# First modulation weights loaded in four column blocks, each block's tiles modulated and multiplied as it lands, tokens loaded first

## The chip, the cores and the metric

The kernel runs on one core of one Trainium2 chip. The metric is the device time of one execution in microseconds (us), from the first to the last instruction. The core has TensorE (PE; its weight loads are listed as PEld), VectorE (DVE), ScalarE (ACT), GpSimd (POOL) and SyncE (SP), which here issues the DMAs. Each engine has its own instruction stream and runs it in order; streams meet at semaphores, so an instruction that waits holds up all that stands behind it in its stream.

## What is computed

One inference step of a two-layer backbone over 512 latent tokens (`x_sample`, modulated by `c`) and 128 context tokens (`x_prompt`, modulated by `c_ctx`), width 1024, all in fp32. Only the first operation of the first layer is touched: tokens are normalised, scaled and shifted by two rows of a modulation that is itself a matrix product, and multiplied by the input projection.

```python
def modulation(cond, w_ada, b_ada):
    m = jax.nn.silu(cond) @ w_ada + b_ada          # w_ada: (1024, 6 * 1024)
    return m.reshape(cond.shape[0], 6, D_MODEL)

def modulate(x, g, shift, scale):
    return rms_norm(x, g) * (1 + scale[:, None, :]) + shift[:, None, :]

for layer in range(DEPTH):
    mc = modulation(c_ctx[None], w_ada[layer], b_ada[layer])
    ml = modulation(c, w_ada[layer], b_ada[layer])
    g = norm_gains[layer]
    hp = modulate(xp, g[0], mc[:, 0], mc[:, 1])
    hs = modulate(xs, g[0], ml[:, 0], ml[:, 1])
    ...                                            # h @ w_in, mixers, residuals, MLP
```

## The kernel before

**Layout.** Activations are held turned: 1024 features in KD = 8 tiles (k = 0 to 7) of 128 partitions, T = 640 tokens along the free dimension. The tokens are two halves of HALF = 320 columns: half (or part) 0 holds latent tokens only, half 1 the rest and the 128 context tokens, which have another scale and shift. Every fp32 matrix product is done as three fp32r matmuls over a split of each operand in a high and a low piece: lo x hi, hi x lo, hi x hi.

**Weights.** A piece of `w_in_ac` (128 output columns, all 8 k tiles, 512 KB) lands in one of four `stage` buffers; ACT copies it to `w_hi` (`act_split`, L566), DVE subtracts to `w_lo` (`dve_split`, L575). A unit is one piece times the tokens: 8 k tiles, two halves, three matmuls of 320 columns, so 48 matmuls. Units 0 to 2 are written by hand in `units_beside` (L863 to L865), units 3 to 19 come from `unit` (L824 to L826). Unit 3 needs the bank of unit 1, so ACT's copy of unit 1's result (L1594); ahead of that copy in ACT's stream stand the copy of unit 0 and the splits of pieces 4 and 5.

**The modulation.** The first two rows of the modulation (shift and scale, 2048 columns of `w_ada`, 8 MB) come as eight row blocks of 1 MB, one for each k (`ada_a`, L699). `ada_step(k)` (L912) is four matmuls of 512 columns with 32 weight columns each, which lie side by side in PE's columns. After the eighth, ACT copies the result (`modrow_a`, L1570), PE turns it (L953), DVE adds the bias (`first_columns`, L2115) and makes the coefficients (L2106).

**The operands.** For half 0 and tile k: DVE `modulate` (L2064), ACT high piece (L1505), DVE low piece (`low`, L2081). For half 1: DVE multiplies by the token factor (L2071), ACT applies scale and shift to the two groups (L1516, two instructions) and copies to the high piece (L1520), DVE subtracts for the low piece (L2088). The token factor itself is ACT's sum of squares (L1559) and root, spread over the partitions by PE (`spread_rows`, L935 and L937). Tokens are turned by PE (`turn_tokens`, L923) and copied by DVE (`turned_out`, L2173 and, for the context, L2175).

**The order of the DMAs.** All go through SP's queue: ident, the vectors (`vrow`, `brow`), `x_sample`, the eight `ada_a` blocks, pieces 0 and 1, `x_prompt`, pieces 2 and 3, small ones, then two slabs for the rest of the modulation (`slab_ac`) and the next pieces. The orders are written out by hand on every engine.

## Time and profile before

| | us |
|---|---|
| median of 3 runs (lowest, highest) | 1739.69 (1739.23, 1740.97) |
| the profiled execution | 1740.12 |
| its span | 1738.3 |
| last `ada_a` block used by PE | 32.8 |
| first product of unit 0 | 41.0 |
| first product of unit 3 | 67.8 |

Share of the span with the engine busy: PE 96%, PEld 86%, DVE 63%, ACT 42%, POOL 12%. The granted TensorE clock averages 0.98 of full speed. Times in the rows are microseconds from the span's start; DMA share is the mean busy share of the 16 DMA engines. A matmul's listed duration overlaps its neighbours', so PE's pace is read from the distance of two starts.

### The profile page before, as it was taken

What the parts mean: (1) busy time and instruction counts of PE and PEld (TensorE: products, weight loads), DVE (VectorE), ACT (ScalarE), POOL (GpSimd) and SP (SyncE); (2) the same over time, 40 slices, a digit from 0 to 9 for tenths busy, and PEclk for the clock granted to TensorE, in tenths of its full rate; (3) what the DMA queues carried; (4) which work ended last, traced back from release to release, by engine and by line L of the source; (5) the groups of instructions that cost most, each with busy time, mean ns of one, the idle gap of its engine ahead of it and who ended that gap; (6) DMA issues with size and microseconds to landing.
All of it is one profiled execution on the core that took longest, in us unless ns stands there. A gap on an engine that the chain in (4) does not pass through costs nothing.

```text
span 1738.3 us, 26413 instructions
## 1 busy us (share of the span) xinstructions
PE 1674.2 (96%) x10650; PEld 1494.3 (86%) x10650; DVE 1102.8 (63%) x1726; ACT 735.0 (42%) x1238; POOL 213.5 (12%) x204
## 2 busy tenths in 40 slices
PE   5999999899999999999999999999999999999997
PEld 3999864689999999999989974445999999999996
DVE  3777666856757777785587647886585653332345
ACT  3433235755653312213345745654475332221333
POOL 0000014432100000000120402443310000000011
PEclk7999999999999999999999989999999999999998
DMA  9455212131556456473412500002154722222231
GB/s 334 155 174 166 82 47 61 29 104 31 149 176 176 121 170 194 122 205 99 116 38 49 149 13 1 1 1 83 52 146 134 206 74 73 73 74 80 79 85 61
DMA packets 266794, 181.63 MB, mean 104 GB/s; under 512 B 26237, under 2 KB 239090, under 8 KB 265650
## 3 DMA queue, kind: packets, MB, share of 16 engines
q1 hardware_dynamic: 266674, 179.96, 35.7%
q8 instruction: 85, 1.39, 0.3%
q14 instruction: 35, 0.29, 0.1%
HBM read 173.75 MB, written 3.62 MB: 102 GB/s over the span
## 4 chain that ended last, share of the span: by engine, by line
PE 81%; DVE 9%; ACT 3%; issue 3%; DMA 2%; SPq 1%; POOL 0%; DVEq 0%; ACTq 0%; POOLq 0%
PE ps L824 21%; PE ps L826 21%; PE ps L825 21%; PE ps L1397 3%; PE ps L1407 2%; DMA ada_a<-in_w_ada 1%; PE ps L990 1%; PE ps L992 1%; PE ps L991 1%; DVE w_lo L575 1%; PE ps L1024 1%; PE ps L1006 1%; PE ps L878 1%; ACT km L1923 1%; ACT w_hi L566 1%
## 5 line engine op out<-in xcount | busy, mean ns | idle before, releaser
L566 ACT ACTIVATE w_hi<-stage 128x1024 fp32r<-128x1024 f32 (+1 forms) x176 | 184.7, 1052 | 615.8 <-PE ps L826 500.1
L575 DVE TENSOR_TENSOR w_lo<-stage,w_hi 128x1024 fp32r<-128x1024 f32 (+1 forms) x176 | 216.8, 1233 | 281.9 <-ACT w_hi L566 281.7
L824 PE MATMUL ps<-hM_hi,w_lo 128*128 128x320 f32 x952 | 295.2, 310 | 0.0
L826 PE MATMUL ps<-hM_hi,w_hi 128*128 128x320 f32 x952 | 294.2, 309 | 0.0
L825 PE MATMUL ps<-hM_lo,w_hi 128*128 128x320 f32 x952 | 294.1, 309 | 0.0
L824 PE MATMUL ps<-h_hi,w_lo 128*128 128x320 f32 x824 | 255.9, 311 | 2.6 <-DVE h_lo L2497 2.6
L826 PE MATMUL ps<-h_hi,w_hi 128*128 128x320 f32 x824 | 254.6, 309 | 0.0
L825 PE MATMUL ps<-h_lo,w_hi 128*128 128x320 f32 x824 | 254.6, 309 | 0.0
L2742 POOL TENSOR_TENSOR rstd<-rstd,sq 128x320 f32<-128x320 f32 x73 | 77.3, 1064 | 960.8 <-ACT sq L1490 959.2
L824 PEld LDWEIGHTS ps<-hM_hi,w_lo 128*128 128x128 f32 x952 | 178.7, 188 | 3.4 <-issue 3.4
L825 PEld LDWEIGHTS ps<-hM_lo,w_hi 128*128 128x128 f32 x952 | 178.7, 188 | 0.1
L826 PEld LDWEIGHTS ps<-hM_hi,w_hi 128*128 128x128 f32 x952 | 178.7, 188 | 0.0
L824 PEld LDWEIGHTS ps<-h_hi,w_lo 128*128 128x128 f32 x824 | 154.6, 188 | 6.8 <-DVE h_lo L2497 3.7
L825 PEld LDWEIGHTS ps<-h_lo,w_hi 128*128 128x128 f32 x824 | 154.7, 188 | 0.0
L826 PEld LDWEIGHTS ps<-h_hi,w_hi 128*128 128x128 f32 x824 | 154.7, 188 | 0.0
L2150 DVE SCALAR_TENSOR_TENSOR acc_mlp<-slab_mlp,csil,acc_mlp 128x512 f32<-128x512 f32 x196 | 134.5, 744 | 0.0
L2480 DVE TENSOR_TENSOR yT<-yT,ps 128x640 f32<-128x640 f32 (+1 forms) x64 | 41.7, 651 | 109.4 <-PE ps L826 108.8
L824 PE MATMUL ps<-hA_hi,w_lo 128*128 128x320 f32 x272 | 84.5, 311 | 1.6 <-ACT oT L1594 1.6
L826 PE MATMUL ps<-hA_hi,w_hi 128*128 128x320 f32 x272 | 84.0, 309 | 0.0
L825 PE MATMUL ps<-hA_lo,w_hi 128*128 128x320 f32 x272 | 84.0, 309 | 0.0
L1975 ACT ACTIVATE pT<-ps 128x512 f32<-128x512 f32 x84 | 49.8, 595 | 56.1 <-PE ps L1397 53.6
L2621 DVE TENSOR_REDUCE w_lo<-ps 128x1 fp32r<-128x512 f32 x64 | 43.4, 678 | 41.5 <-PE ps L1303 41.4
(412 smaller groups left out, 3525.8 us busy)
## 6 DMA issues: line engine op xcount, KB each, us to landing
stage<-in_w_mlp_out SPq DMA_DIRECT2D x83, 512.0 KB, 4.2
stage<-in_w_mlp_in SPq DMA_DIRECT2D x80, 512.0 KB, 4.6
slab_mlp<-in_w_ada SPq DMA_DIRECT2D x28, 1024.0 KB, 5.3
stage<-in_w_in_ac SPq DMA_DIRECT2D x28, 512.0 KB, 3.9
slab_ac<-in_w_ada SPq DMA_DIRECT2D x12, 1024.0 KB, 6.1
ada_a<-in_w_ada SPq DMA_DIRECT2D x8, 1024.0 KB, 16.6
stage<-in_w_out_ac SPq DMA_DIRECT2D x8, 512.0 KB, 4.1
stage<-in_w_out_c SPq DMA_DIRECT2D x8, 512.0 KB, 4.3
```

Source lines behind the costliest of these rows:

```text
L566: nc.scalar.activation(hi_place(n)[:, 0:width], stage[:, n % STAGE, 0:width], ACT.Copy)\
L575: nc.vector.tensor_tensor(lo_place(n)[:, 0:width], stage[:, n % STAGE, 0:width], hi_place(n)[:, 0:width].bitcast(F32), ALU.subtract).then_ ...
L824: mm(out, lo[:, k], xh, start=j == 0, stop=False)
L825: mm(out, hi[:, k], xl, start=False, stop=False)
L826: last = mm(out, hi[:, k], xh, start=False, stop=j == k_tiles - 1)
L1397: mm(ps[:, 2 + n % 2, :], km[0:97, h, P * kb:P * (kb + 1)], q, start=True, stop=True).then_inc(m_s, 1)
L1407: last = mm(ps[64 * e:64 * e + 64, 4 + (p + 1) % 2, :], vm[:, KEY_ORDER[ki], HD * h:HD * (h + 1)], pT[:, (n + e) % P_RING, :], start=ki == ...
L1975: f(pT[:, n % P_RING, :], ps[:, 2 + n % 2, :], ACT.Exp).then_inc(m_e, 1)
L2150: last = stt(acc, w, c, acc, ALU.mult, ALU.add)
L2480: tt(y_, y_, p_, ALU.add).then_inc(dve_evac, 1)
L2621: nc.vector.tensor_reduce(peak[p % 2][:, 96 + j:97 + j], ps[:, ROUGH_BANK[a], :], AX.X, ALU.max, negate=True)\
L2742: sub(rstd[:, half(s)], rstd[:, half(s)], sq[:, k % 2, half(s)], ALU.add).then_inc(added[s], 1)
```

## The change

`w_ada`'s first 2048 columns come in four column blocks of 2 MB instead of eight row blocks. Block q holds the 256 columns of the shift row and the 256 of the scale row that tiles 2q and 2q + 1 need. `ada_step(q)` is now 16 matmuls of 256 columns, two side by side, and four of these steps replace one pass. After step q + 1 the row is copied, turned and added for that block alone, then tiles 2q + 2 and 2q + 3 are made and multiplied (`quarter_products`). Unit 2 joins from block 1 on. The tokens, the context's too, are loaded ahead of everything. The spread token factors are copied by ACT from PSUM to `rstd`. The normalised tiles of half 1 have two buffers instead of four. The low pieces of half 1 move from DVE to POOL (`first_low`). `ada_a` lies elsewhere, so SP waits for the last step before it issues the first two slabs, and all later pieces stand behind that wait.

```diff
-ADA_START = 1
+ADA_START = 4
+ADA_Q = 256
...
-        [ada_a] = lay(64, ("ada_a", [P, KD, 4 * GRP], F32))
-        [modrow_a] = lay(130, ("modrow_a", [P, GRP], F32))
-        [cwide] = lay(62, ("cwide", [P, KD, 32], F32))
+        [ada_a] = lay(22, ("ada_a", [P, ADA_START, KD, 2 * ADA_Q], F32))
+        [modrow_a] = lay(88, ("modrow_a", [P, 2 * ADA_Q], F32))
+        [cwide] = lay(90, ("cwide", [P, KD, 32], F32))
...
         def spread(name, s):
 
+            if name == "in0":
+                return rstd[:, half(s)]
...
-            n = k % 4
+            n = k % 2 + 2 * s if name == "in0" else k % 4
...
+            sp.dma_start(xtok[:, 0:NB, :], i["x_sample"][0].rearrange("(b p) d -> p b d", p=P)).then_inc(x_in, 16)
+            sp.dma_start(xtok[:, NB, :], i["x_prompt"][0]).then_inc(prompt_in, 16)
             sp.dma_start(ident[:], i["c_ident"]).then_inc(const_in, 16)
...
             sp.dma_start(brow[:], i["b_ada"].rearrange("l (f p) -> (l f) p", p=P)).then_inc(rows_in, 16)
-            sp.dma_start(xtok[:, 0:NB, :], i["x_sample"][0].rearrange("(b p) d -> p b d", p=P)).then_inc(x_in, 16)
-            for k in range(KD):
-                sp.dma_start(ada_a[:, k, :], i["w_ada"][0, P * k:P * (k + 1), 0:4 * GRP]).then_inc(ada_in[k], 16)
-            for j in range(2):
-                load_piece("ac", j)
-            sp.dma_start(xtok[:, NB, :], i["x_prompt"][0]).then_inc(prompt_in, 16)
-            for j in range(2, STAGE):
-                load_piece("ac", j)
+            def load_ada(q):
+
+                columns = i["w_ada"][0][:, 0:2 * D].rearrange("(k p) (e m) -> p k e m", p=P, e=2)
+                for e in range(2):
+                    sp.dma_start(ada_a[:, q, :, ADA_Q * e:ADA_Q * (e + 1)], columns[:, :, e, ADA_Q * q:ADA_Q * (q + 1)])\
+                        .then_inc(ada_in[q], 16)
+
+            load_ada(0)
+            load_piece("ac", 0)
+            load_piece("ac", 1)
+            load_ada(1)
+            load_piece("ac", 2)
+            load_ada(2)
+            load_ada(3)
+            load_piece("ac", 3)
             sp.dma_start(kpos[:], i["c_kpos"]).then_inc(decay_in, 16)
             sp.dma_start(dec[:, 0:8], i["ret_decay_fwd"].to_broadcast([P, NH])).then_inc(decay_in, 16)
             sp.dma_start(dec[:, 8:16], i["ret_decay_bwd"].to_broadcast([P, NH])).then_inc(decay_in, 16)
+            table_rows()
+            sp.dma_start(dist[:], i["c_dist"]).then_inc(dist_in, 16)
+            sp.wait_ge(ada_done, ADA_START)
             load_slab(0)
             load_slab(1)
-            table_rows()
-            sp.dma_start(dist[:], i["c_dist"]).then_inc(dist_in, 16)
             n = 2
...
-            def units_beside(units, part, beside=None):
+            def quarter_products(q, part, units):
 
                 pe.wait_ge(w_lo_done, units[-1] + 1)
-                together = KD - 2 if part else KD
-                steps = [(k, units) for k in range(together)]
-                steps += [(k, (g,)) for g in units for k in range(together, KD)]
-                for k, at_once in steps:
-                    if beside and k in beside:
-                        beside[k]()
+                for k in (2 * q, 2 * q + 1):
                     h_ready("in0", part)(k, k)
-                    for g in at_once:
+                    for g in units:
+                        first = k == 0 if g < 2 else k == 2
                         hi, lo = [w.rearrange("p (k m) -> p k m", k=KD)[:, k] for w in (hi_place(g), lo_place(g))]
                         out, xh, xl = ps[:, first_bank(g) + part, 0:HALF], hA_hi[:, k, half(part)], hA_lo[:, k, half(part)]
-                        mm(out, lo, xh, start=k == 0, stop=False)
+                        mm(out, lo, xh, start=first, stop=False)
                         mm(out, hi, xl, start=False, stop=False)
                         last = mm(out, hi, xh, start=False, stop=k == KD - 1)
                         if part and k == KD - 1:
...
-            def ada_step(k):
-
-                pe.wait_ge(ada_in[k], 16)
-                for j in range(4):
-                    last = mm(ps[32 * j:32 * j + 32, 0, :], cwide[:, k, :], ada_a[:, k, GRP * j:GRP * (j + 1)],
-                              start=k == 0, stop=k == KD - 1)
-                if k == KD - 1:
-                    last.then_inc(ada_done, 1)
+            def ada_step(q):
+
+                pe.wait_ge(ada_in[q], 32)
+                rows, cols = 64 * (q % 2), slice(ADA_Q * (q // 2), ADA_Q * (q // 2 + 1))
+                for k in range(KD):
+                    for e in range(2):
+                        last = mm(ps[rows + 32 * e:rows + 32 * e + 32, 4, cols], cwide[:, k, :],
+                                  ada_a[:, q, k, ADA_Q * e:ADA_Q * (e + 1)], start=k == 0, stop=k == KD - 1)
+                last.then_inc(ada_done, 1)
+
+            def turn_modulation(q):
+
+                pe.wait_ge(modrow_done, q + 1)
+                if q:
+                    pe.wait_ge(mod_out, q)
+                rows, first = slice(64 * (q % 2), 64 * (q % 2) + 64), ADA_Q * (q // 2)
+                for n in range(2):
+                    last = nc.tensor.transpose(ps[:, 5, P * q + 64 * n:P * q + 64 * (n + 1)],
+                                               modrow_a[rows, first + P * n:first + P * (n + 1)], ident[rows, rows])
+                last.then_inc(mod_t, 1)
...
             for j in range(8):
                 turn_tokens(j)
-            pe.wait_ge(c_ready, 1)
-            for k in range(6):
-                ada_step(k)
-            pe.wait_ge(x_out, 8)
-            spread_rows(0)
-            ada_step(6)
-            ada_step(7)
-            pe.wait_ge(modrow_done, 1)
-            for n in range(4):
-                last = nc.tensor.transpose(ps[:, 1, P * n:P * (n + 1)], modrow_a[:, P * n:P * (n + 1)], ident[:])
-            last.then_inc(mod_t, 1)
             pe.wait_ge(prompt_in, 16)
             for j in range(8, 10):
                 turn_tokens(j)
-
-
-            pe.wait_ge(mod_out, ADA_START)
             sums_at_unit, turns_at_unit = {8: 0, 14: 1, 19: 2}, {9: 0, 15: 1}
 
-            units_beside((0, 1), 0, {6: lambda: spread_rows(1)})
+            pe.wait_ge(c_ready, 1)
             pe.wait_ge(x_out, 10)
-            units_beside((2,), 0)
-            units_beside((0, 1, 2), 1)
+            ada_step(0)
+            spread_rows(0)
+            spread_rows(1)
+            turn_modulation(0)
+            for q in range(ADA_START):
+                units = (0, 1, 2) if q else (0, 1)
+                quarter_products(q, 0, units)
+                if q == 1:
+                    pe.wait_ge(rstd_done[0], 1)
+                    pe.wait_ge(rstd_done[1], 1)
+                    quarter_products(0, 0, (2,))
+                if q < ADA_START - 1:
+                    ada_step(q + 1)
+                quarter_products(q, 1, units)
+                if q == 1:
+                    quarter_products(0, 1, (2,))
+                if q < ADA_START - 1:
+                    turn_modulation(q + 1)
...
+            def spread_copy(s):
+
+                act.wait_ge(spread_done[s], 1)
+                f(rstd[:, half(s)], ps[:, 6 + s, 0:HALF], ACT.Copy).then_inc(rstd_done[s], 1)
+
+            def modulation_row(q):
+
+                act.wait_ge(ada_done, q + 1)
+                rows, cols = slice(64 * (q % 2), 64 * (q % 2) + 64), slice(ADA_Q * (q // 2), ADA_Q * (q // 2 + 1))
+                f(modrow_a[rows, cols], ps[rows, 4, cols], ACT.Copy).then_inc(modrow_done, 1)
+
             act.wait_ge(x_in, 16)
             for b in range(NB):
                 token_squares(b)
+            act.wait_ge(prompt_in, 16)
+            token_squares(NB)
             token_roots(0)
-            act.wait_ge(ada_done, 1)
-            f(modrow_a[:], ps[:, 0, :], ACT.Copy).then_inc(modrow_done, 1)
-            act_split(act, 0)
-            act_split(act, 1)
-            for k in range(KD):
-                operand("in0", 0, k)
-                if k == 1:
-                    act.wait_ge(prompt_in, 16)
-                    token_squares(NB)
-                    token_roots(1)
-            act.wait_ge(x_t, 10)
-            act_split(act, 2)
-            for k in range(KD):
-                operand("in0", 1, k)
-                if k == 3:
-                    act_split(act, 3)
+            token_roots(1)
+            modulation_row(0)
+            spread_copy(0)
+            spread_copy(1)
+            for q in range(ADA_START):
+                if q in (0, 1):
+                    act_split(act, 2 * q)
+                for s in range(2):
+                    operand("in0", s, 2 * q)
+                    operand("in0", s, 2 * q + 1)
+                    if s == 0 and q == 0:
+                        act_split(act, 1)
+                    if s == 0 and q < ADA_START - 1:
+                        modulation_row(q + 1)
+            act_split(act, 3)
...
-                if k >= 4:
-                    dve.wait_ge(h_lo_done[s], KD * MOD_NO[name] + k - 3)
+                back = 2 if name == "in0" else 4
+                if k >= back:
+                    dve.wait_ge(h_lo_done[s], KD * MOD_NO[name] + k - back + 1)
...
-            for j in range(8):
+            for j in range(10):
                 turned_out(j)
             token_roots(0)
-            first_columns()
-            modulate("in0", 0, 0)
-            modulate("in0", 0, 1)
-            dve_split(dve, 0)
-            low("in0", 0, 0)
-            dve_split(dve, 1)
-            for k in range(2, KD):
+            token_roots(1)
+            for q in range(ADA_START):
+                first_columns(q)
+                k = 2 * q
                 modulate("in0", 0, k)
-                low("in0", 0, k - 1)
-                if k == 4:
-                    turned_out(8)
-                    turned_out(9)
-                    token_roots(1)
-            low("in0", 0, KD - 1)
-            dve_split(dve, 2)
-            dve.wait_ge(h_lo_done[0], KD)
-            for k in range(KD):
+                modulate("in0", 0, k + 1)
+                if q == 0:
+                    dve_split(dve, 0)
+                low("in0", 0, k)
+                low("in0", 0, k + 1)
                 modulate("in0", 1, k)
-                if k:
-                    low("in0", 1, k - 1)
-                if k == 5:
-                    dve_split(dve, 3)
-            low("in0", 1, KD - 1)
+                modulate("in0", 1, k + 1)
+                if q == 0:
+                    dve_split(dve, 1)
+                if q == 1:
+                    dve_split(dve, 2)
+            dve_split(dve, 3)
...
+            def first_low(k):
+
+                pool.wait_ge(h_hi_done[1], k + 1)
+                sub(hA_lo[:, k, half(1)], norm_place("in0", 1, k), hA_hi[:, k, half(1)].bitcast(F32), ALU.subtract)\
+                    .then_inc(h_lo_done[1], 1)
+
+            for k in range(KD):
+                first_low(k)
```

On PE, around the first column blocks. `ada_a` is the modulation block, `modrow_a` its result's copy, `hA` the operand, 0 and 1 behind `h_lo_done` the half. Before, all modulation steps end ahead of the first product:

```order
L912 MATMUL ps<-ada_a,cwide 32x512 [waits ada_in7]
L912 MATMUL ps<-ada_a,cwide 32x512 x3
L953 MATMUL ps<-ident,modrow_a 128x128 [waits modrow_done]
L953 MATMUL ps<-ident,modrow_a 128x128 x3
L923 MATMUL ps<-ident,xtok 128x128 [waits x_out,prompt_in]
L923 MATMUL ps<-ident,xtok 128x128 x3
L923 MATMUL ps<-ident,xtok 128x128 [waits x_out]
L923 MATMUL ps<-ident,xtok 128x128 x3
L863 MATMUL ps<-hA_hi,w_lo 128x320 [waits h_lo_done0,w_lo_done,mod_out]
```

After, from the last product of block 0's half 0:

```order
L875 MATMUL ps<-hA_hi,w_hi 128x320
L924 MATMUL ps<-ada_a,cwide 32x256 [waits ada_in1]
L924 MATMUL ps<-ada_a,cwide 32x256 x15
L873 MATMUL ps<-hA_hi,w_lo 128x320 [waits h_lo_done1,w_lo_done]
```

and, 11 matmuls on, the turning of block 1 and its first product:

```order
L875 MATMUL ps<-hA_hi,w_hi 128x320
L935 MATMUL ps<-ident,modrow_a 128x64 [waits mod_out,modrow_done]
L935 MATMUL ps<-ident,modrow_a 128x64
L873 MATMUL ps<-hA_hi,w_lo 128x320 [waits h_lo_done0,w_lo_done]
```

Step 1 now stands between half 0's and half 1's products of block 0, and the turning of block 1 behind both.

On ACT, in the same place. Before:

```order
L1570 ACTIVATE modrow_a<-ps 128x512 [waits ada_done]
L566 ACTIVATE w_hi<-stage 128x1024 [waits w_in0]
L566 ACTIVATE w_hi<-stage 128x1024 [waits w_in1]
L1505 ACTIVATE hA_hi<-nt,mod 128x320 [waits h_full0] x2
L1559 ACTIVATE sq,rs<-xtok 128x1024 [waits prompt_in]
```

After:

```order
L1529 ACTIVATE hA_hi<-nt,mod 128x320 [waits h_full0] x2
L570 ACTIVATE w_hi<-stage 128x1024 [waits w_in1]
L1598 ACTIVATE modrow_a<-ps 64x256 [waits ada_done]
L1540 ACTIVATE nt<-nt,mod,coef 128x192 [waits h_full1]
L1540 ACTIVATE nt<-nt,mod,coef 128x128
L1544 ACTIVATE hA_hi<-nt 128x320 [waits affine_done]
L1540 ACTIVATE nt<-nt,mod,coef 128x192 [waits h_full1]
L1540 ACTIVATE nt<-nt,mod,coef 128x128
L1544 ACTIVATE hA_hi<-nt 128x320 [waits affine_done]
L570 ACTIVATE w_hi<-stage 128x1024 [waits w_in2]
L1529 ACTIVATE hA_hi<-nt,mod 128x320 [waits h_full0] x2
```

The copy of block 1's row, which waits for PE's step 1, now stands ahead of half 1's operands of block 0.

On DVE, from the turned row of a block to the next. After:

```order
L2154 TENSOR_TENSOR mod<-ps,badaT 128x2x2 [waits mod_t]
L2154 TENSOR_TENSOR mod<-ps,badaT 128x2x2
L2160 SCALAR_TENSOR_TENSOR coef<-mod,vecT 128x2 [waits mod_out]
L2160 SCALAR_TENSOR_TENSOR coef<-mod,vecT 128x2
L2101 SCALAR_TENSOR_TENSOR nt<-xT,coef,rstd 128x320 [waits h_lo_done0,rstd_done0,dve_chain]
L2101 SCALAR_TENSOR_TENSOR nt<-xT,coef,rstd 128x320 [waits h_lo_done0,rstd_done0]
L2118 SCALAR_TENSOR_TENSOR hA_lo<-nt,mod,hA_hi 128x320 [waits h_hi_done0] x2
L2108 TENSOR_TENSOR nt<-xT,rstd 128x320 [waits h_lo_done1,rstd_done1] x2
L579 TENSOR_TENSOR w_lo<-stage,w_hi 128x1024 [waits w_hi_done]
```

Before:

```order
L2115 TENSOR_TENSOR mod<-ps,badaT 128x16 [waits mod_t]
L2115 TENSOR_TENSOR mod<-ps,badaT 128x16
L2106 SCALAR_TENSOR_TENSOR coef<-mod,vecT 128x8 [waits mod_out]
L2106 SCALAR_TENSOR_TENSOR coef<-mod,vecT 128x8
L2064 SCALAR_TENSOR_TENSOR nt<-xT,coef,ps 128x320 [waits rstd_done0,dve_chain]
L2064 SCALAR_TENSOR_TENSOR nt<-xT,coef,ps 128x320 [waits rstd_done0]
L575 TENSOR_TENSOR w_lo<-stage,w_hi 128x1024 [waits w_hi_done]
```

The bias and coefficient instructions now come four times, and in block 1 the split of piece 2 stands at the end of the block's DVE work.

## Rows read from the trace of the kernel before

**Rows 1.** The chain of waits to 130 us: start, duration, what

```profile
8.05 24.68 DMA ada_a<-in_w_ada
32.78 1.98 PE ps L912 x8
34.79 0.60 ACT modrow_a L1570
35.44 1.13 PE ps L953 x4
36.59 0.27 DVE mod L2115 x2
...
37.16 1.00 DVE nt L2064 x2
```

**Rows 2.** Timeline 0 to 90 us, tokens and vectors: start, duration, instruction

```profile
0.73 0.41 SPq L688 DMA_DIRECT2D ident<-in_c_ident  x1
...
3.69 0.43 SPq L697 DMA_DIRECT2D xtok<-in_x_sample  x1
...
11.69 5.80 PE L923 MATMUL ps<-ident,xtok 128*128 128x128 f32 x32 [5.97 <-DMA xtok<-in_x_sample]
...
12.85 7.67 DVE L2173 COPY xT<-ps 128x512 f32<-128x512 f32 x8 [5.82 <-PE ps L923]
...
43.58 1.28 DVE L2175 COPY xT<-ps 128x512 f32<-128x512 f32 x2
```

**Rows 3.** Timeline 0 to 90 us, PE's modulation steps and second spread

```profile
17.42 2.80 PE L912 MATMUL ps<-ada_a,cwide 128*32 128x512 f32 x24
...
48.69 0.98 PE L935 MATMUL ps<-ident,rs 128*128 128x48 f32 x8
...
49.72 0.39 PE L863 MATMUL ps<-hA_hi,w_lo 128*128 128x320 f32 x1
```

**Rows 4.** Timeline 0 to 90 us, products at either clock

```profile
42.20 0.47 PE L864 MATMUL ps<-hA_lo,w_hi 128*128 128x320 f32 x1
...
42.47 0.47 PE L865 MATMUL ps<-hA_hi,w_hi 128*128 128x320 f32 x1
...
48.10 0.31 PE L865 MATMUL ps<-hA_hi,w_hi 128*128 128x320 f32 x1
...
48.25 0.31 PE L863 MATMUL ps<-hA_hi,w_lo 128*128 128x320 f32 x1
```

**Rows 5.** Timeline 0 to 90 us, an operand of half 0 and a split

```profile
47.14 0.54 DVE L2081 SCALAR_TENSOR_TENSOR hA_lo<-nt,mod,hA_hi 128x320 fp32r<-128x320 f32 x1
...
47.25 0.56 ACT L1505 ACTIVATE hA_hi<-nt,mod 128x320 fp32r<-128x320 f32 x1 [0.36 <-DVE nt L2064]
...
48.79 1.22 DVE L575 TENSOR_TENSOR w_lo<-stage,w_hi 128x1024 fp32r<-128x1024 f32 x1 [0.39 <-ACT w_hi L566]
```

**Rows 6.** Timeline 62 to 68.5 us, an operand of half 1, then unit 3

```profile
61.73 0.92 ACT L1516 ACTIVATE nt<-nt,mod,coef 128x192 f32<-128x192 f32 x2
...
62.68 0.47 ACT L1520 ACTIVATE hA_hi<-nt 128x320 fp32r<-128x320 f32 x1
...
65.07 2.00 ACT L566 ACTIVATE w_hi<-stage 128x1024 fp32r<-128x1024 f32 x2
...
67.81 0.38 PE L824 MATMUL ps<-hA_hi,w_lo 128*128 128x320 f32 x1 [1.62 <-ACT oT L1594]
```

**Rows 7.** Groups of POOL by shape: count, busy us, mean ns, idle before

```profile
L2742 POOL TENSOR_TENSOR rstd<-rstd,sq 128x320 f32<-128x320 f32 x73 | 77.3, 1064 | 960.8 <-ACT sq L1490 959.2
```

**Rows 8.** Windows: stretch, length, PE busy (instructions), granted clock, DMA share, GB/s

```profile
30.00:35.00 5.00, 4.29 (x19) 0.50 1.13 322
41.00:46.00 5.00, 5.00 (x19) 0.50 1.05 400
...
1194.00:1196.00 2.00, 0.00 (x0) 1.00 0.98 276
1196.00:1198.00 2.00, 1.97 (x6) 0.62 0.08 23
```

More of the change, by code:

```diff
@@ L399, in build @@
         prompt_in = sem("prompt_in")
-        ada_in = [sem(f"ada_in{k}") for k in range(KD)]
+        ada_in = [sem(f"ada_in{q}") for q in range(ADA_START)]
+        spread_done = [sem(f"spread_done{s}") for s in range(2)]
         csil_zero = sem("csil_zero")
@@ L922, in turn_tokens @@
                 for n in range(4):
-                    last = nc.tensor.transpose(ps[:, 4 + (j if j < 8 else j + 2) % 4, P * n:P * (n + 1)],
+                    last = nc.tensor.transpose(ps[:, 4 + j % 4, P * n:P * (n + 1)],
                                                xtok[:, b, P * (4 * g + n):P * (4 * g + n + 1)], ident[:])
@@ L929, in spread_rows @@
                 pe.wait_ge(rs_ready[s], 1)
-                out = spread("in0", s)
+                out = ps[:, 6 + s, 0:HALF]
                 cols = (slice(0, 40), slice(40, 64))[s]
@@ L937, in spread_rows @@
                     last = mm(out[:, TL - HALF:], rs[:, 0, NB:NB + 1].to_broadcast([P, P]), ident[:], start=True, stop=True)
-                last.then_inc(rstd_done[s], 1)
+                last.then_inc(spread_done[s], 1)
             pe.wait_ge(x_in, 16)
@@ L2108, in coefficients, with first_columns @@
                     link(last)
-            def first_columns():
-                dve.wait_ge(mod_t, 1)
-                cols = ps[:, 1, :].rearrange("p (n j c) -> p j n c", n=4, j=4)
+            def first_columns(q):
+                dve.wait_ge(mod_t, q + 1)
+                cols = ps[:, 5, P * q:P * (q + 1)].rearrange("p (n e c) -> p e n c", n=2, e=2)
                 for g in range(2):
-                    last = tt(mod[:, 0, 0:16, g].rearrange("p (j n) -> p j n", j=4), cols[:, :, :, g],
-                              badaT[:, 0, 0:16].rearrange("p (j n) -> p j n", j=4), ALU.add)
+                    to, bias = [x.rearrange("p (e q n) -> p e q n", e=2, q=ADA_START)[:, :, q, :]
+                                for x in (mod[:, 0, 0:16, g], badaT[:, 0, 0:16])]
+                    last = tt(to, cols[:, :, :, g], bias, ALU.add)
                 last.then_inc(mod_out, 1)
-                dve.wait_ge(mod_out, 1)
-                coefficients(0, SCALE1)
+                dve.wait_ge(mod_out, q + 1)
+                for g in range(2):
+                    gain = vecT[:, ROW_GAIN + 8 * A1 + 2 * q:ROW_GAIN + 8 * A1 + 2 * q + 2]
+                    m = mod[:, 0, 8 * SCALE1 + 2 * q:8 * SCALE1 + 2 * q + 2, g]
+                    last = stt(coef[:, 0, A1, 2 * q:2 * q + 2, g], m, 1.0, gain, ALU.add, ALU.mult)
+                link(last)
             def mod_pair(p, bank):
@@ L2169, in turned_out @@
                 dve.wait_ge(x_t, j + 1)
-                src, tiles = ps[:, 4 + (j if j < 8 else j + 2) % 4, :], slice(4 * g, 4 * g + 4)
+                src, tiles = ps[:, 4 + j % 4, :], slice(4 * g, 4 * g + 4)
                 if b < NB:
```

## Prediction

> **What bounds the kernel now.** I read three views in this order: the chain of waits, the timeline of the first 70 us, and the windows with the granted clock. Behind unit 3 nothing in the change touches an instruction, and PE is busy 96% of the span, so I measure everything by one moment, M, the start of unit 3. It is 67.8 us before [rows 6], and what M gains or loses I carry to the end one to one. Ahead of M the chain is: the last row block of `ada_a` lands, PE's step on it starts at 32.8, the row is copied at 34.8, turned at 35.4, and DVE makes the columns at 36.6 and the first tiles at 37.2 [rows 1]. The first product starts at 41.0 behind two weight splits. Up to 32.8 the DMAs are the bound: PE needs all 8 MB before it can modulate one tile. From 41.0 on PE is fed: 144 products in a row. So the head has two parts, 41 us of waiting for data and 27 us of dense products, and the change cuts the first by breaking up the second.
>
> **Up to the first product.** `x_sample` starts to be used 8.0 us after its issue at 3.69; it is now issued at 0.73 in place of ident [rows 2], so it is there at 8.7. But the turning also waits for ident and the vectors, which now queue behind 2.6 MB of tokens. The lower bound is 8.7 (they cost nothing), the upper 12 (0.5 MB of context tokens at some 320 to 400 GB/s [rows 8] is 1.3 to 1.6 us, and a DMA's own latency on top). I take 11.1, hardly earlier than the 11.7 of before. From there DVE is the pace: 1.16 to its first copy, 7.67 for eight, 1.28 for the two of the context [rows 2], which gives 21.2.
>
> `ada_step(0)`: three steps of four 512-column matmuls took 2.80 us [rows 3], 0.87 each if the overlap at the end is taken off. The new step is 8 x 2 matmuls of 256 columns, two abreast instead of four: each pair is half a row-block step, 0.43, so 3.5 us a block at full clock and 7.0 at half. The four together are 14 us of PE where eight were 7. Lower bound: the eight-step total, 7.0 / 4 = 1.7 a block, if narrow matmuls hide in each other; upper: no overlap, 7 at full clock. I take 3.5, since four abreast of 512 columns scale to it. The two spreads are 1.0 each at full clock [rows 3] (49.7 less 48.7), turning is 0.65 (half of 1.13, plus latency) [rows 1]. That is 21.2 + 3.5 + 2.0 + 0.65 = 27.4.
>
> Then DVE: columns and coefficients 0.57, two tiles 1.0 [rows 1], split of piece 0 1.13, two low pieces 0.92, two tiles of half 1 0.88, split of piece 1 1.22 [rows 5], for PE waits for the second split: 5.8 with the hop. **First product at 33.2 instead of 41.0**: 7.8 us ahead.
>
> **From the first product to M.** Here the order of the streams decides. PE runs: products (block q, half 0), step q + 1, products (q, half 1), turning q + 1. ACT's copy of row q + 1 stands ahead of its half-1 operands of block q. So, for q = 0, 1, 2:
>
> 1. Step q + 1, 3.5, with nothing beside it on PE.
> 2. PE then waits: row copy 0.4 (of 0.60 for twice the columns [rows 1]), affine 0.92 and high piece 0.47 [rows 6], low piece on POOL 1.06 [rows 7], hops 0.15. That is 3.0. DVE did the low piece in 0.5; POOL's price is from an addition of the same shape, and I take it between 0.85 and 1.7.
> 3. Products of half 1; then turning 0.65.
> 4. PE waits again: 0.57 columns, 0.5 tile, 0.56 high, 0.54 low [rows 1, 5] is 2.2. In block 1 unit 2 joins, and its split stands behind a second low piece 0.46, two tiles 0.88 and itself 1.22: 4.8.
>
> Sum at full clock: products 144 x 0.147 = 21.2 [rows 4]; steps 3 x 3.5 = 10.5; turnings 2.0; waits of point 2, 9.0; of point 4, 2.2 + 2.2 + 4.8 = 9.2; half 1's tiles of block 0 and of the last block come a little later than PE could take them, 1.2. Together 53.1, so the products end at 86.3. Before, unit 0 ended 1.7 us ahead of the rest and ACT's copy and two splits (2.00 [rows 6]) ran beside them; now all three units end within 1.3 us, so 2.5 pass instead of 1.6. M = 88.8, **21 us later than before**.
>
> **The clock.** That sum holds at full speed. Before, the first 5 us of products ran at half clock: 0.50 over 41 to 46, starts 0.27 apart against 0.15 later [rows 4, 8]. Steps and spreads did not lift it: 4.29 us busy of 5 at 30 to 35, still 0.50 [rows 8]. And 2.4 us without PE work around 1194 to 1196 dropped it, 1.00 and then 0.62 over the next two [rows 8]. The new head has six waits of 2.2 to 4.8 us, so each run of products begins low or falls soon. All at half clock: products 144 x 0.27 = 38.9 (17.7 more), steps 10.5 more, small ones 0.6 more, 1.2 of pacing gone: 27.6 more, M = 116.4, 48.6 later.
>
> Between the ends: the runs between two steps or waits are 12, 12, 24, 24, 18, 18 and 36 products, at half clock 3.2 to 9.7 us. With a rise after some 4 to 5 us of products, as from 41 to 46, only the two runs of 24 and the last get a tail at full clock: 1 + 1 + 2.5 us saved, and 3.5 if the step behind the first stays up. I grant 4 more, because the clock had also stayed up from 20 to 25 through steps with gaps. 12 of 27.6: M = 104.4, 36.6 later.
>
> The Trainium skill (TensorE: Matmul & The Clock Gate, section HAM oscillation — how this bites in real kernels) describes a loop of short matmul bursts with a wait in each and finds that every burst starts cold; it advises keeping the k tiles contiguous. That rule speaks against this change, and by it the time would be the all-low end. Rows 8 agree in direction; whether every burst starts low no row here shows.
>
> **What costs nothing.** Each block lands long before it is asked for: at the 322 GB/s of mixed loads [rows 8] the 12.8 MB up to block 3 take 40 us, and step 3 starts at about 70. The slabs and pieces behind SP's new wait have the 14 us or more from step 3 to the end of the products, and pieces 4 and 5 with 2 MB of slabs are 3.1 MB, 10 us; beyond that, PE would wait. ACT's copies of the token factors, 1 us, lie beside the turning. POOL is idle there.
>
> The Trainium skill (SBUF — State Buffer, section Who interferes with whom) says that a VectorE instruction with two SBUF inputs and a GpSimd one block each other. By it a low piece on POOL can be held by DVE's tiles, up to 1.2 us each; no row here shows a subtraction on POOL in this place, and DVE mostly waits for PE by then.
>
> **The rivals.**
>
> - *Clock stays up.* Same chain, M = 88.8: 1739.7 + 21 = 1761. For it: the waits are mostly under 3 us; against it, the fall at 1196.
> - *Worse chain.* Two column groups don't overlap (7 us more a step at half clock, three times) or the clock stays low throughout: M = 116 to 137, 1788 to 1808.
> - *PE hides the waits.* If the order let PE do the next step while ACT and POOL work, only PE's own work counts: 33.2 + 21.2 + 10.5 + 2.0 + 2.5 = 69.4, 1741.3, no change. Against it: the row copy and the half-1 operands are in one ACT stream behind PE's step.
> - *The DMA is the bound, and the change works (faster).* Block 3 there at 40, step 3.5, its last waits 6.5, 36 products 5.3, 2.5 to M: 57.8, 10 us earlier, 1729.7. It needs the first three blocks' 108 products and two steps, 22.9 us, to fit between 33.2 and 50, so it wants steps under 1 us each and none of the six waits. It decides from a loop of 5 us a block; I count 15.
> - *It doesn't move the first product.* If the vectors land late or the steps are at half clock from the start, the 7.8 us of lead shrink by up to 5. Inside my range.
>
> **How the numbers follow.** The profiled execution took 1740.12 us with a span of 1738.3, and the median of the runs is 1739.69, so the trace can stand for it within 0.1%. Forecast: 1739.7 + 36.6 = 1776.3, I say 1776; chance 0.62 for 1767 to 1787. Clock up 0.17; worse chain 0.12; no change 0.05; faster 0.04. The range takes in the clock-up case less 4 us for a short POOL price and tokens at 8.7, and the low end of the worse chain: 1757 to 1792. A difference under 0.2% (3.5 us) is about what a measurement can't tell from none. Faster by more 0.04, within 0.05, slower by more 0.91.
>
> **What would show it.** Right: first product at 31 to 36; PE gaps of about 3 us behind each step, ended by POOL's low pieces, and of 2 to 5 behind each turning, ended by DVE; steps of 3.5 or 7 us; granted clock mostly 0.50 between 33 and 100; unit 3 at 95 to 115; everything behind it shifted by the same. Wrong: products of a block that follow on each other without gaps, or DMA-ended waits at the later steps (then the loads are the bound and the time is lower), or a difference that comes or goes behind unit 3.

## The result, and the profile after

| | us |
|---|---|
| median of the kernel after (lowest, highest) | 1774.45 (1771.07, 1774.84) |
| its profiled execution, and the span | 1774.84, 1773.1 |
| median of the kernel before, run beside it | 1739.6 |
| ratio after to before, 95% interval | 1.0198 [1.0185, 1.0211] |
| unit 3 starts (M), before and after | 67.81, 100.38 |

The change costs 34.8 us, and the forecast was 1776 (1757 to 1792). M moved by 32.6 us, the span by 34.8: nearly everything is lost before unit 3. The granted clock is 0.979 over the span where it was 0.982, and PE's busy share falls from 96% to 95%, so neither average tells what happened. The timeline does. First its rows for PE up to the first product (start, duration, engine, line, instruction, and in brackets the wait before it and what ended it); they answer to [rows 2, 3]:

```profile
11.47 0.37 PE L914 MATMUL ps<-ident,vrow 85*128 85x85 f32 x1 [11.47 <-DMA brow<-in_b_ada]
...
22.43 5.20 PE L924 MATMUL ps<-ada_a,cwide 128*32 128x256 f32 x32 [2.34 <-issue]
27.57 1.98 PE L957 MATMUL ps<-ident,rs 128*128 128x80 f32 x16
...
29.77 0.33 PE L935 MATMUL ps<-ident,modrow_a 64*128 64x64 f32 x2
...
35.74 0.63 PE L873 MATMUL ps<-hA_hi,w_lo 128*128 128x320 f32 x1 [5.64 <-DVE w_lo L579]
```

The first product is 5.3 us earlier than the 41.0 of before. From there to unit 3, these are all of PE's steps and all its waits over 0.2 us:

```profile
39.23 3.65 PE L924 MATMUL ps<-ada_a,cwide 128*32 128x256 f32 x32
...
45.86 0.39 PE L873 MATMUL ps<-hA_hi,w_lo 128*128 128x320 f32 x1 [2.97 <-POOL hA_lo L2791]
...
54.34 0.63 PE L873 MATMUL ps<-hA_hi,w_lo 128*128 128x320 f32 x1 [4.76 <-DVE w_lo L579]
...
60.48 3.65 PE L924 MATMUL ps<-ada_a,cwide 128*32 128x256 f32 x32
...
66.96 0.61 PE L873 MATMUL ps<-hA_hi,w_lo 128*128 128x320 f32 x1 [2.83 <-POOL hA_lo L2791]
...
74.80 0.39 PE L873 MATMUL ps<-hA_hi,w_lo 128*128 128x320 f32 x1 [2.45 <-DVE hA_lo L2118]
...
77.60 3.65 PE L924 MATMUL ps<-ada_a,cwide 128*32 128x256 f32 x32
...
84.21 0.61 PE L873 MATMUL ps<-hA_hi,w_lo 128*128 128x320 f32 x1 [2.96 <-POOL hA_lo L2791]
...
91.09 0.61 PE L873 MATMUL ps<-hA_hi,w_lo 128*128 128x320 f32 x1 [2.45 <-DVE hA_lo L2118]
...
100.38 0.38 PE L838 MATMUL ps<-hA_hi,w_lo 128*128 128x320 f32 x1 [2.49 <-ACT oT L1630]
```

Seven waits, 20.9 us, where PE in the kernel before, once its products have begun, waits only 1.62 us, ahead of unit 3 [rows 6]. Three stand behind the steps, three behind the turnings, one ahead of unit 3. What is in a wait behind a step is shown by the chain of waits, the first of the three:

```profile
39.30 3.61 PE ps L924 x32
42.94 0.38 ACT modrow_a L1598
43.34 0.94 ACT nt L1540 x2
44.30 0.48 ACT hA_hi L1544
44.85 0.87 POOL hA_lo L2791
45.86 0.39 PE ps L873
```

ACT had waited 9.71 us for step 1, with half 1's operands behind that wait; only then could it start on what PE needed next. The clock, in windows (stretch, length, PE busy with its instructions, granted clock, DMA share, GB/s), which answer to [rows 8]:

```profile
22.00:24.00 2.00, 1.57 (x8) 0.55 1.10 350
24.00:26.00 2.00, 2.00 (x14) 0.59 1.11 339
26.00:28.00 2.00, 2.00 (x20) 1.00 1.18 304
34.00:36.00 2.00, 0.26 (x1) 0.50 1.09 348
46.00:48.00 2.00, 2.00 (x9) 0.53 0.00 0
54.00:56.00 2.00, 1.66 (x6) 0.50 0.00 0
66.00:68.00 2.00, 1.04 (x4) 0.65 0.04 8
84.00:86.00 2.00, 1.79 (x7) 0.50 1.05 407
90.00:92.00 2.00, 0.91 (x3) 0.62 1.22 291
102.00:104.00 2.00, 2.00 (x10) 0.50 0.61 133
```

It fell to 1.2 GHz in or just behind the 5.64 us ahead of the first product and six of the seven waits above (not at the 2.45 us ahead of 74.80), stayed there for 3 to 6 us and rose again to 2.4. Two windows of the list (46 and 54) also show the DMAs at 0 GB/s: all four column blocks had long landed and were never waited for.

### The profile page after: what moved, and what is told of

Its sections match the earlier page's. It is cut to its first block, busy times and chain, and to the rows that moved or that the text cites. A ratio compares the mean times of both kernels' runs of the same rounds, so it can differ in the third digit from the quotient of the medians.

```text
span 1773.1 us, 26579 instructions
## 1 busy us (share of the span) xinstructions
PE 1686.5 (95%) x10718; PEld 1506.6 (85%) x10718; DVE 1100.7 (62%) x1730; ACT 736.3 (42%) x1243; POOL 220.1 (12%) x212
## 4 chain that ended last, share of the span: by engine, by line
PE 82%; DVE 9%; ACT 3%; issue 3%; DMA 2%; POOL 1%; SPq 0%; DVEq 0%; ACTq 0%; POOLq 0%
PE ps L838 20%; PE ps L839 20%; PE ps L840 20%; PE ps L1421 3%; PE ps L1431 2%; DMA stage<-in_w_mlp_out 1%; DVE w_lo L579 1%; PE ps L1014 1%; PE ps L1015 1%; PE ps L1016 1%; PE ps L1048 1%; PE ps L924 1%; PE ps L888 1%; PE ps L1030 1%; ACT w_hi L570 1%
```

## The experiments

Ratios are to the kernel before, run beside each kernel; its median was 1738.7 beside kernels 1 to 4, 1738.3 beside 5, 6, 8 and 9, and 1739.5 beside 7 and 10. A time is the median of a kernel's runs; M and all rows come from one profiled execution of it. The stretch behind M, the span less M, is 1670.5 us before and 1672.7 after; how far such a difference can be trusted is shown at the end of the last section.

**1. The row copy behind half 1's operands.** One word on ACT:

```diff
-                    if s == 0 and q < ADA_START - 1:
+                    if s == 1 and q < ADA_START - 1:
                         modulation_row(q + 1)
```

> ACT's copy of row q + 1 stands behind half 1's operands of block q instead of ahead of them; nothing else changes. M is the start of unit 3: 67.8 us in the kernel before, 100.4 after the change. If the three waits behind the modulation steps (2.97, 2.83 and 2.96 us in the changed kernel) come from this order, they go: M 88 to 92, 1761 to 1766 us, and the step is followed by products at once. If they come from POOL being slow or from the loads, the gaps of some 3 us stay, only with POOL as their end: M 99 to 101, 1773 to 1775 us.

1759.33 us, 1.0113 [1.0096, 1.0130]; M 87.25. All three waits behind the steps are gone; the three behind the turnings stand as they were:

```profile
50.37 0.58 PE L873 MATMUL ps<-hA_hi,w_lo 128*128 128x320 f32 x1 [4.76 <-DVE w_lo L579]
...
65.71 0.38 PE L873 MATMUL ps<-hA_hi,w_lo 128*128 128x320 f32 x1 [2.45 <-DVE hA_lo L2118]
...
77.71 0.55 PE L873 MATMUL ps<-hA_hi,w_lo 128*128 128x320 f32 x1 [2.45 <-DVE hA_lo L2118]
```

Time and M are both a little below what was expected. M came 13.1 us sooner, of which 8.8 are the three waits. The remaining 4.3 agree with fewer falls of the clock: before M, PE runs products for some 11 us at 1.2 GHz where it was 21, and a product takes 0.27 us there against 0.15. One place in one stream cost 15 of the 35 us.

**2. The turning ahead too.** On top of 1:

```diff
                 if q < ADA_START - 1:
                     ada_step(q + 1)
+                    turn_modulation(q + 1)
                 quarter_products(q, 1, units)
...
-                if q < ADA_START - 1:
-                    turn_modulation(q + 1)
```

> As the run with the row copied behind half 1's operands, and PE turns row q + 1 right behind its step, ahead of half 1's products of block q, so that the next block's columns and tiles are made beside these products. If the order of the streams is the cause, the waits behind the turnings (4.76, 2.45, 2.45 us) shrink to under 1 us each, at the price of about 0.6 us per turning for the row's copy, and the clock stays up for longer: M 76 to 82, 1749 to 1755 us. If the time is PE's own doubled work instead, M stays at 88 to 92 as in the other run.

1756.06 us, 1.0096 [1.0081, 1.0111]; M 80.26. M is as expected, the time 1 us above. The half-1 products now cover DVE's and ACT's way to the next tiles: two of the waits behind turnings are gone and 4.76 became 2.79. In exchange PE waits 0.48 us for each row copy. A new wait appeared, which in the kernel after was hidden. On ACT, behind SP's wait for the last step:

```profile
76.65 1.06 ACT L570 ACTIVATE w_hi<-stage 128x1024 fp32r<-128x1024 f32 x1 [0.57 <-DMA stage<-in_w_in_ac]
78.47 1.06 ACT L570 ACTIVATE w_hi<-stage 128x1024 fp32r<-128x1024 f32 x1 [0.77 <-DMA stage<-in_w_in_ac]
```

PE waited 4.05 us for unit 3 instead of 2.49, and the clock was low again from 80.3 to 85.7. So M gained 7.0 us and the time only 3.3. Nor are the 7.0 all the turning's: 1.5 of them came before the first product (34.36 where kernel 1 had 35.82), where nothing was changed. Step 0 ran at full clock there, behind the same wait as in kernel 1, where it took 5.33:

```profile
22.60 3.65 PE L924 MATMUL ps<-ada_a,cwide 128*32 128x256 f32 x32 [2.34 <-issue]
```

**3. The low piece back on DVE.** In the kernel after, `first_low` is removed from POOL and `low("in0", 1, k)` stands behind half 1's tiles on DVE.

> Half 1's low pieces go back from POOL to DVE, in the changed kernel. Theory (the chain of waits): each of the first tiles of a block is 0.86 - 0.50 = 0.36 us earlier, three to four times: M 98.9 to 99.5, 1772 to 1774 us. Rival (POOL and its shared way to SBUF with DVE hold up the chain): M falls by 3 us or more, below 1771.

1770.77 us, 1.0184 [1.0169, 1.0199]; M 95.83. The waits behind the steps are 2.56, 2.42 and 2.55 us, 0.4 each shorter, as POOL's 0.87 against DVE's 0.5 gives: 1.2 us in all. By its numbers this is what was expected of the rival (M down by 3 us or more, below 1771), but the rows give POOL only those 1.2. M moved by 4.6, of which 1.7 came before the first product (34.01), where nothing was changed: step 0 ran at full clock there, 3.65 us, and at the low one in the kernel after, 5.20. The other 1.6 go with the clock too: behind 63.68 it stayed up where it had fallen behind 66.96. The same instructions take either way into step 0, which may be part of why executions of the kernel after spread from 1771 to 1775; only one of them has a profile.

**4. The clock alone.** In the kernel after, PE's waits are filled with products of `ident` with itself, into columns of a bank that nothing reads at that time; they compute nothing that is used. `warm(n, c)` issues n of them into the columns from c on:

```diff
             turn_modulation(0)
+            warm(22, 256)
...
                     ada_step(q + 1)
+                    warm(10, 0 if q else 256, slice(64 * (q % 2), 64 * (q % 2) + 64))
...
                     turn_modulation(q + 1)
+                    warm(9 if q else 18, 0 if q else 256)
```

> The changed kernel with matmuls on ident put into PE's waits, written to a part of PSUM that nobody reads: 22 ahead of the first product, 10 of half width behind each modulation step, 18, 9 and 9 behind the turnings, about 0.21 us each at full clock. They compute nothing that is used. If the low clock is a cause of its own, worth about 10 us between the first product and M, the granted clock stays at 1.00 from the second block on and M falls to 89 to 94: 1763 to 1769 us. If the waits alone are the cause and the clock follows without a price, M stays or grows by the 1 to 2 us by which the fillers overrun: 1774 to 1777 us.

1763.47 us, 1.0140 [1.0125, 1.0155]; M 91.89, with every data wait still in its place: the first product behind each step and each turning comes as long after it as in the kernel after, to 0.13 us. Windows as above:

```profile
34.00:36.00 2.00, 1.47 (x13) 1.00 1.10 349
46.00:48.00 2.00, 2.00 (x17) 1.00 0.03 8
54.00:56.00 2.00, 2.00 (x18) 1.00 0.00 0
66.00:68.00 2.00, 1.99 (x18) 1.00 0.00 0
```

The clock's own share is thus 8.5 us of M and 10 us of the time (the ratio went from 1.0198 to 1.0140; about 1 of the 1.5 between them is unit 3, low after and not here). The other 24 us of M are waits and work in the chain.

**5. Half a step.** `for k in (0, 2, 5, 7)` in `ada_step`; it leaves out half of the modulation's product.

> The kernel after, with 4 of the 8 row groups in each step: half of the product of the modulation is left out, so that each step has 16 products of 32 columns and not 32. Theory (a step in the stream costs its own length and no more): 1.8 us less for each of steps 1 to 3 and 1.8 to 2.6 us less for step 0, 7 to 8 us in all, time 1766.5 to 1768.5, by the clock some 2 us to either side. Rival (what counts is the number of times the stream is broken, and the steps' length hides part of ScalarE's and VectorE's work that is waited for): the waits behind the turnings (4.8, 2.4, 2.4 us) grow by what the steps lose, 1772 to 1775.

1767.41 us, 1.0163 [1.0148, 1.0179]. Steps 2 and 3 take 1.92 us each instead of 3.65, and the six waits are the same to the hundredth: 2.97, 4.76, 2.83, 2.45, 2.96, 2.45. A step hides nothing of the other engines' work that PE waits for here; it costs its length. By length alone that is 5.6 us up to unit 3 (2.2 in step 0, less 0.6 as the spreads behind it now run low, 0.5 in step 1 at low clock, 1.7 each in steps 2 and 3). M came 3.7 us sooner, since the clock fell in other places, and the median 7.0, where 7 to 8 were expected. That the time met the expectation is in part luck: 3.6 us of the difference between the two profiled spans lie behind M, where nothing was changed.

**6. The tokens first, alone,** in the kernel before: `x_sample` and `x_prompt` are issued ahead of ident and the vectors.

> The kernel before with one part of the change alone: the two token transfers go ahead of the vectors on SP. The tokens then land about 2 us sooner and the vectors at about 11.4 us; the modulation still follows its weights, which land last. Theory (the loads bound the start of the kernel before, and the order of the first ones decides nothing): within 1 us of the kernel before. Rival (the order alone is part of the loss, as step 0 waits for the vectors): 1 to 3 us slower.

1739.13 us, 1.0000 [0.9990, 1.0009]. No change. The vectors were there at 11.84, the first product came at 39.40 and M at 66.05. That is 1.6 and 1.8 us sooner than in the profile of the kernel before, in which the clock was at 0.50 from 30 to the first product; the medians show none of it.

**7. The vectors half back,** in the kernel after: between `x_sample` and `x_prompt`.

> The kernel after, with the vectors read between the two token transfers instead of behind both: one part of the change taken half back. Theory (step 0 waits for the tokens' turnings and these for the vectors): the vectors land some 1.3 us sooner, and unit 3 and the time come 1 to 2 us sooner, 1772.5 to 1773.5, by the clock some 2 us to either side. Rival (the order of the first loads decides nothing here either, as in the kernel before with the tokens first): within 0.5 us of the kernel after, 1774 to 1775.

1771.74 us (1770.46 to 1774.86), 1.0192 [1.0178, 1.0206]. The vectors landed at 10.46 instead of 11.44 and the first product came 0.9 us sooner, at 34.87, but M is 100.38 again: step 1 began at the low clock and took 4.12 us instead of 3.65, and of the runs of products behind it three took 0.1 to 0.3 us longer. The median is 2.7 us lower, the intervals overlap. Neither theory is settled by it; what it shows is that a microsecond gained at the front can be lost to the clock before it reaches the end.

**8. Everything in its cover.** On top of 2: step 1 goes ahead of the first product, splits 0 and 1 ahead of the columns on ACT and DVE, split 2 into block 0, the vectors between the tokens, and pieces 4 and 5 ahead of SP's wait:

```diff
             turn_modulation(0)
+            ada_step(1)
...
-                if q < ADA_START - 1:
+                if 0 < q < ADA_START - 1:
                     ada_step(q + 1)
+                if q < ADA_START - 1:
                     turn_modulation(q + 1)
...
+            load_piece("ac", STAGE)
+            load_piece("ac", STAGE + 1)
             sp.wait_ge(ada_done, ADA_START)
```

> e2_turn_ahead with what still stood ahead of unit 3 in it moved too: step 1 goes ahead of the first product; the splits of the operand (0 and 1) go ahead of the columns; the vectors are read between the two token transfers; and pieces 4 and 5 of the adaptation weights are read ahead of SP's wait for the last step, which in e2 kept ScalarE's splits waiting for DMAs (0.57 and 0.77 us at 76.7 and 78.5). Theory (a sum of small ends at the row's start, of which each can be moved): e2's unit 3 stood at 80.3; less about 3.0 + 2.8 us of waits behind step 1 and its turning, 4.05 + 1.3 us ahead of unit 3, and up to 2 us of the clock: unit 3 at 66 to 70, time 1738 to 1742. Rival (the steps are work that the kernel before had under its loads, and in the stream they cost their full 4 x 3.65 us whatever stands around them): unit 3 at 74 to 78, time 1748 to 1752.

1743.76 us, 1.0023 [1.0010, 1.0036]; M 67.99, the kernel before's to 0.2 us, the time some 2 us above what I expected and 0.2% above the kernel before. The first product is at 32.29. By M, column blocks are thus no slower by themselves; they are also no faster, for the four steps cost 14.6 us of PE at full clock. What each of the moves gives was not run by itself.

**9. Steps 2 and 3 as one,** four products of 32 columns abreast:

```diff
+            def ada_pair():
+
+                pe.wait_ge(ada_in[2], 32)
+                pe.wait_ge(ada_in[3], 32)
+                for k in range(KD):
+                    for q in (2, 3):
+                        for e in range(2):
+                            r = 64 * (q % 2) + 32 * e
+                            last = mm(ps[r:r + 32, 4, ADA_Q:2 * ADA_Q], cwide[:, k, :],
+                                      ada_a[:, q, k, ADA_Q * e:ADA_Q * (e + 1)], start=k == 0, stop=k == KD - 1)
+                last.then_inc(ada_done, 2)
```

Both rows are then turned together.

> e3_all, and steps 2 and 3 done as one: four products of 32 columns abreast on the array where a step has two, so that the pair should take about the time of one (3.7 us instead of 7.3), if the four run abreast as the four tiles of a product do. Theory: 3.6 us less than e3_all before unit 3, and one waiting less: 62 to 66, time 1733 to 1738, the kernel before being 1738.7 to 1739.6. Rival (a 32-column product costs its issue, not its columns): the pair takes 7.3 us as the two steps did, time as e3_all within 1 us.

1736.30 us, 0.9989 [0.9980, 0.9998]; M 63.40. The pair takes what one step did, twice the products in the same time:

```profile
28.85 3.65 PE L926 MATMUL ps<-ada_a,cwide 128*32 128x256 f32 x32
...
41.85 3.66 PE L938 MATMUL ps<-ada_a,cwide 128*32 128x256 f32 x64
```

**10. And the first step at full clock.** On top of 9, nine idle products ahead of step 0:

```diff
+            for _ in range(9):
+                mm(ps[:, 0, 0:P], ident[:], ident[:], start=True, stop=True)
             pe.wait_ge(c_ready, 1)
```

> e6_pair with nine products of the identity with itself (into a bank that holds nothing yet) in TensorE's wait of 2.36 us between the tokens and step 0. In e6_pair, as in all kernels of this study with step 0 at 21 to 22, the granted clock fell in that wait and step 0 took 5.3 us instead of 3.65. Theory (the clock falls for the wait alone): step 0 takes 3.65 us, and unit 3 and the time come 1.5 to 1.8 us sooner, 1734 to 1735. Rival (step 0 runs low for its own narrow products, or the column blocks then bound the start): step 0 at 5 us or step 1 waiting for its block, time as e6_pair's 1736.3 within 0.5 us.

1735.74 us, 0.9979 [0.9970, 0.9988]: faster than the kernel before by 3.7 us. PE's timeline:

```profile
21.25 3.65 PE L926 MATMUL ps<-ada_a,cwide 128*32 128x256 f32 x32 [0.36 <-issue]
...
41.48 3.66 PE L938 MATMUL ps<-ada_a,cwide 128*32 128x256 f32 x64 [1.14 <-DMA ada_a<-in_w_ada]
...
63.04 0.38 PE L840 MATMUL ps<-hA_hi,w_lo 128*128 128x320 f32 x1 [2.49 <-ACT oT L1660]
```

Step 0 took 3.65 us instead of 5.33, with the granted clock at 1.00 throughout, so narrow products alone do not bring it down. That the fill kept it up one profile can't show, for in kernels 2 and 3 step 0 took 3.65 without it. M moved only 0.4 us, for now the pair waits 1.14 us for its block: there the loads are the bound at last, as the rival had it. The time lies between the two expectations, and against kernel 9 the gain is within the intervals.

## Why the prediction was right

The kind of loss, its place and its size came out as forecast; the main terms:

| step | forecast | after |
|---|---|---|
| copies of the tokens end | 21.2 | 22.3 |
| step 0 | 3.5 | 5.20 |
| first product | 33.2 | 35.74 |
| steps in the stream | 3.5 | 3.65 |
| waits behind steps | 3.0, three times | 2.97, 2.83, 2.96 |
| waits behind turnings | 4.8, 2.2, 2.2 | 4.76, 2.45, 2.45 |
| gap ahead of unit 3 | 2.5 | 2.49 |
| M | 104.4 | 100.38 |

- **Up to the first product** I was 2.5 us too early. 1.1 of it is the vectors, which landed at 11.44 behind the tokens, with the way to the token turnings that stands behind them on PE (12.45 where I had 11.1 for all of it). 1.7 is step 0 at low clock.
- **The order of the streams** was the cause of the waits behind steps: kernel 1 takes them away with one word. The waits behind turnings were it too in kernel 2: two went and the third fell to 2.79. The low piece on POOL took 0.86 to 0.88 us, near the 0.85 end of my bound and not the 1.06 of the addition. The Trainium skill (SBUF — State Buffer, section Who interferes with whom) says that a VectorE instruction with two SBUF inputs contends with a GpSimd one that reads SBUF; with no tile on DVE beside it (its two, 0.80 to 0.89 us, were done before the row copy) no row here puts that to the test.
- **The clock** had the right sign and too large a size. Between the first product and M, PE ran products for some 21 us at 1.2 GHz, which at 0.27 us each instead of 0.15 loses between 9 and 10; I had 15.6 (27.6 less 12). Kernel 4 measures 8.5. The error is in a sentence that I read out of [rows 8], that steps do not lift the clock: 22 to 26 of the windows above holds nothing but step 0 at 0.55 and 0.59, and it is 1.00 at 26; steps 1 to 3 took 3.65 us each, the length at full clock. Of the eight bursts from 35.74 to unit 3, five started low (their first product takes 0.61 to 0.63 us); at 45.86, 74.80 and 100.38 it takes 0.38 or 0.39, and at the first and the last of these the clock fell only then. The all-low end, 116.4, was not near. In the loop that the Trainium skill describes (TensorE: Matmul & The Clock Gate, section HAM oscillation — how this bites in real kernels) every burst starts cold, but each of its waits is longer than most of these: here the two bursts behind waits of 4.76 and 5.64 us agree with it, and of the six behind 2.45 to 2.97 us three do.
- **Behind M** I had carried the shift on one to one. POOL's MEMSET of `bias` comes 190.0 us behind M before, 191.6 after and 190.7 in kernel 4: the clock was low again in unit 3, at 102 to 104, behind the gap of 2.49, which costs some 1 to 1.6 us. That term was missing. The rest of the difference is not the change's: see the last section.
- **Part of the closeness is luck.** The clock was put 7.1 us too high. Against that stood 2.5 us too little up to the first product, 0.7 in the steps and waits after it, and 2.2 behind M that were put at nothing; so 1776 lies nearer to 1774.45 than its terms do to theirs.
- **The loads** were not the bound, as forecast. What I gave 14 us of cover had it only because the waits were long: with the waits gone (kernel 2) SP's wait for the last step delayed ACT's splits.
- **Of the rivals,** the closest was the clock that stays up, 1761: kernel 4 is that case, at 1763.5. The one that has PE hide the waits, 1741.3, comes nearest in kernel 8, at 1743.8, in which more was moved; against it I had put the order of ACT's stream, and that order was one word and 13.1 us of M.

The path of M tells what the 32.6 us were, each with what came before it in place: 13.1 the row copy's place, 5.5 the turning's, and 13.8 step 1, the splits, the vectors and the loads together, and 4.6 more by pairing, which takes it below the kernel before. (Kernel 2's step 0 at full clock, 1.5 us, is taken out of its 7.0 and put back into the 12.3 between kernels 2 and 8; kernel 8's ran low again.) The parts were taken away in this order only; another would share them out differently, as the clock's share is in all of them.

## What to carry to other kernels

Before a load is cut into pieces so that work can start sooner, write down each engine's stream for one piece and look for the instruction that waits for another engine while what that engine needs next stands behind it; here that cost 13 us of M, where the earlier first product had gained 5.3. A dense stretch behind a long load may be worth more than an early start, since each break costs its own length and then the clock. And a start that is cut up pays only as far as the extra work it makes (14.6 us of steps for 7) is also packed, here by four narrow products abreast.

## What the runs showed of the hardware

- Products of 32 weight columns alone, 256 columns wide, brought the granted clock back up: 0.55 and 0.59 over 22 to 26, 1.00 over 26 to 28. It had fallen behind a wait of 2.34 us. Behind the same wait it stayed up in kernels 2 and 3, without any change there.
- Two such products side by side and four abreast take the same 3.65 us for 8 row groups. The row-block step of the kernel before, four abreast of 512 columns, is 0.87 us a row group [rows 3]; 8 x 0.46 is half of that per row group, for half the columns, with two places used or four. In these three cases the length goes by the columns streamed and not by the places; one place alone was not run.
- The column blocks came at 339 to 350 GB/s (the windows at 22, 24 and 34), the row blocks of the kernel before at 422 and 424 (windows 20 to 30 and 12 to 20 of its trace, that of the loads alone). The column blocks' packets are 1 KB where the row blocks' rows are 8 KB. PE never waited for a column block until kernel 10, where the lower rate may be part of the 1.14 us; no run tests it.
- A subtraction of 128 x 320 to fp32r took POOL 0.87 us and DVE about 0.5.
- One profiled execution carries chance of some us, much of it far from the change. Over all twelve profiles the span less M lies between 1669.1 and 1674.9 us. About 955 us behind M there is a wait of 2.28 us for ScalarE, and the clock is low behind it for longer in one execution than in another. The kernel before, then kernel 5 in the same place (windows as above):

```profile
1020.00:1025.00 5.00, 2.72 (x16) 0.74 0.00 0
1025.00:1030.00 5.00, 4.72 (x21) 0.50 0.01 3
1030.00:1035.00 5.00, 5.00 (x31) 0.50 0.00 0
```

```profile
1050.00:1055.00 5.00, 2.73 (x21) 0.88 0.00 0
1055.00:1060.00 5.00, 4.72 (x22) 0.50 0.01 3
1060.00:1065.00 5.00, 5.00 (x55) 0.94 0.00 0
```

  POOL's sixth copy to `qB` comes 977.0 us behind M before and 977.4 after, 975.2 in kernel 5, 975.6 in kernel 6 (in which nothing behind the loads was changed) and 979.9 in kernel 2. So M, and not the span of one execution, is what the parts above are measured by, and the medians decide between kernels. M carries chance as well: 1.5 to 1.7 us by the clock of step 0 (kernels 2 and 3), 1.8 in kernel 6.
